# A chunked state-space scan: order of the mixture in VectorE's queue, size of a fill, and place of four products

## What is computed

```
acum = cumsum(a in the chunk)
seg = exp(where(tri, acum_i - acum_j, -inf))
cb = einsum('bnlgd,bnsgd->bnlsg', cc, bc)
y_diag = einsum('bnlsgr,bnsgrp->bnlgrp', cb[..., None] * seg, xc)
def step(state, inp):
    y_off = einsum('blgd,bgrpd,blgr->blgrp', c_i, state, exp(a_i))
    state = state * exp(a_last) + einsum('bsgd,bsgr,bsgrp->bgrpd', b_i, exp(a_last - a_i), x_i)
y = (y_diag + y_off) + d_skip[:, None] * xs
y = y * silu(z)        # and then an rmsnorm of each group of 512 columns
```

## Time and profile before

| | |
|---|---|
| median of 3 runs | 3552.8 us (3549.34 to 3553.31) |
| the profiled execution | 3547.36 us, of which the profile's span is 3545.5 us |
| share of busy time | TensorE 88%, VectorE 36%, ScalarE 28%, GpSimd 10% |
| mean granted TensorE clock | 0.936 of full |
| the preparing stage | about 2896 to 2917 us from the span's start |
| the scan | about 2917 to 3033.5 us |

### The profile page before, as it was taken

One profiled execution on the slowest core, in us unless ns is written; L12 is line 12 of the kernel. 1 busy time (PEld: TensorE's weight loads), 2 busy tenths in 40 slices (PEclk: granted clock), 3 DMA queues, 4 the chain that ended last, 5 costly groups with the idle time before them and its releaser, 6 DMA issues. The chain is left out here.

```text
span 3545.5 us, 45023 instructions
## 1 busy us (share of the span) xinstructions
PE 3116.1 (88%) x18464; PEld 2397.2 (68%) x18464; DVE 1277.1 (36%) x1505; ACT 990.9 (28%) x1456; POOL 362.8 (10%) x226
## 2 busy tenths in 40 slices
PE   6987658878758999998878999999999987789999
PEld 4975643333217888786776888788879764678887
DVE  3237651111124332335344332333232556433322
ACT  3125410000013221334224221422234443432222
POOL 2971000000000000100101000100010007110000
PEclk8999878988978999998899999999999999899999
DMA  6523268999973333220013332333323210323322
GB/s 229 166 88 144 63 275 343 427 428 428 428 284 83 95 96 106 72 83 16 2 60 83 95 95 103 88 95 95 103 68 102 83 38 2 101 55 95 95 96 88
DMA packets 301955, 487.06 MB, mean 137 GB/s; under 512 B 15618, under 2 KB 259805, under 8 KB 288495
## 3 DMA queue, kind: packets, MB, share of 16 engines
q1 hardware_dynamic: 297034, 467.35, 37.9%
q10 hardware_dynamic: 2468, 9.20, 0.6%
q0 software_dynamic: 2304, 8.39, 0.6%
HBM read 457.62 MB, written 27.28 MB: 137 GB/s over the span
## 5 line engine op out<-in xcount | busy, mean ns | idle before, releaser
L436 PE MATMUL psum_banks<-u_high,f_ffn_w_high 128*128 128x512 f32 x1408 | 548.6, 390 | 0.7 <-DVE f_ffn_w_low L2761 0.7
L437 PE MATMUL psum_banks<-u_low,f_ffn_w_high 128*128 128x512 f32 x1408 | 548.2, 389 | 0.0
L438 PE MATMUL psum_banks<-u_high,f_ffn_w_low 128*128 128x512 f32 x1408 | 548.1, 389 | 0.0
L2744 DVE TENSOR_TENSOR f_ffn_w_low<-weight_pieces,f_ffn_w_high 128x2048 fp32r<-128x2048 f32 x128 | 293.5, 2293 | 403.2 <-ACT f_ffn_w_high L2705 403.2
L2705 ACT ACTIVATE f_ffn_w_high<-weight_pieces 128x2048 fp32r<-128x2048 f32 x128 | 244.0, 1906 | 325.6 <-PE psum_banks L438 322.0
L436 PEld LDWEIGHTS psum_banks<-u_high,f_ffn_w_high 128*128 128x128 f32 x1408 | 264.6, 188 | 59.4 <-issue 4.2
L438 PEld LDWEIGHTS psum_banks<-u_high,f_ffn_w_low 128*128 128x128 f32 x1408 | 264.6, 188 | 55.0
L437 PEld LDWEIGHTS psum_banks<-u_low,f_ffn_w_high 128*128 128x128 f32 x1408 | 264.6, 188 | 54.4
L436 PE MATMUL psum_banks<-f_ffn_w_high,f_hidden_high 128*128 128x512 f32 x704 | 274.7, 390 | 3.6 <-issue 3.6
L438 PE MATMUL psum_banks<-f_ffn_w_high,f_hidden_low 128*128 128x512 f32 x704 | 274.0, 389 | 0.0
L437 PE MATMUL psum_banks<-f_ffn_w_low,f_hidden_high 128*128 128x512 f32 x704 | 273.9, 389 | 0.0
(11 more groups left out here) (651 smaller groups left out, 5572.0 us busy)
## 6 DMA issues: line engine op xcount, KB each, us to landing
expert_ring<-in_expert_w_gate SPq DMA_DIRECT2D x32, 2048.0 KB, 34.8
expert_ring<-in_expert_w_up SPq DMA_DIRECT2D x32, 2048.0 KB, 35.5
expert_ring<-in_expert_w_down SPq DMA_DIRECT2D x32, 2048.0 KB, 39.6
weight_pieces<-in_ffn_w_gate SPq DMA_DIRECT2D x88, 512.0 KB, 4.0
weight_pieces<-in_ffn_w_up SPq DMA_DIRECT2D x88, 512.0 KB, 5.3
weight_pieces<-in_ffn_w_down SPq DMA_DIRECT2D x88, 512.0 KB, 3.9
weight_pieces<-in_odd_w_in SPq DMA_DIRECT2D x20, 1024.0 KB, 5.4
mix_in_mod_w<-in_w_ada SPq DMA_DIRECT2D x32, 512.0 KB, 3.8
```

The costliest lines, as they stand in the source:

```text
L436: nc.tensor.matmul(out, lhs.high, rhs.high, start=start, stop=False, skip_group_check=True)
L437: nc.tensor.matmul(out, lhs.high, rhs.low, start=False, stop=False, skip_group_check=True)
L438: return nc.tensor.matmul(out, lhs.low, rhs.high, start=False, stop=stop, skip_group_check=True)
L2744: nc.vector.tensor_tensor(w.low[:, j], raw[:, j], w.high[:, j].bitcast(F32), ALU.subtract).then_inc(w_low, 1)
```

## The change

`own_x` isn't made by VectorE at the scan's start but by GpSimd in the preparing stage, into the free first half of the weight buffer. The fill at the scan's start clears only the first half's states. In VectorE's list of the scan, the mixture of unit 0 is made ahead of the loop and the mixture of unit n + 1 at the end of unit n, behind `advance(n, 1)`. The semaphore `own_ok` goes. The whole diff:

```diff
--- before.py
+++ after.py
@@ -3549,7 +3549,7 @@
 SSD_R = SSD_H // SSD_G
 
 
-def ssd_inputs(k, u_t, w_dt, b_dt, head, bc_t, xx, b_tok, xs, decay, ends):
+def ssd_inputs(k, u_t, w_dt, b_dt, head, bc_t, xx, b_tok, xs, decay, ends, own_x):
 
 
     nc = k.nc
@@ -3609,6 +3609,12 @@
                 last_mm = nc.tensor.matmul(k.ps[:, 2, (2 + half) * n:(3 + half) * n], pick, g, start=True, stop=True)
             last_mm.then_inc(sums_mm, 1)
             turns(range(15, JOBS))
+
+        @block.gpsimd
+        def _(pool):
+            for g in range(SSD_G):
+                nc.gpsimd.tensor_tensor(own_x[:, g], k.c("half_ident").unsqueeze(1).to_broadcast([P, SSD_R, CHUNK]),
+                                        head[:, 1, g * SSD_R:(g + 1) * SSD_R].unsqueeze(2).to_broadcast([P, SSD_R, CHUNK]), ALU.mult)
 
         @block.scalar
         def _(eng):
@@ -3674,7 +3680,7 @@
             nc.vector.tensor_tensor(flat(decay["rest"]), last[:], dt[:], ALU.mult).then_inc(small, 1)
 
 
-def ssd_scan(k, y, b_tok, bc_t, decay, ends, xs, skip, z, squares):
+def ssd_scan(k, y, b_tok, bc_t, decay, ends, xs, own_x, z, squares):
 
 
 
@@ -3687,8 +3693,8 @@
     with Stage(nc, "ssd") as s:
         state = s.sb("state", [P, SSD_G, 2, W])
         seg, mix = s.sb("seg", [P, 2, R, CHUNK]), s.sb("mix", [P, 2, R, CHUNK])
-        cb, own_x = s.sb("cb", [P, U, CHUNK]), s.sb("own_x", [P, SSD_G, R, CHUNK])
-        cb_mm, cb_ok, seg_mm, own_ok = s.sem("cb_mm"), s.sem("cb_ok"), s.sem("seg_mm"), s.sem("own_ok")
+        cb = s.sb("cb", [P, U, CHUNK])
+        cb_mm, cb_ok, seg_mm = s.sem("cb_mm"), s.sem("cb_ok"), s.sem("seg_mm")
         seg_ok, decayed, mixed, first_mm = s.sem("seg_ok"), s.sem("decayed"), s.sem("mixed"), s.sem("first_mm")
         upd_mm, diag_mm, off_mm, s_ok, y_ok = (s.sem(n) for n in ("update_mm", "diag_mm", "off_mm", "state_ok", "y_ok"))
         faded, faded_ok, scaled = s.sb("faded", [P, 2, W]), s.sem("faded_ok"), s.sem("scaled")
@@ -3832,10 +3838,7 @@
 
         @block.vector
         def _(v):
-            nc.vector.memset(state[:], 0.0).then_inc(s_ok, 1)
-            for g in range(SSD_G):
-                nc.vector.tensor_tensor(own_x[:, g], k.c("half_ident").unsqueeze(1).to_broadcast([P, R, CHUNK]),
-                                        skip[:, g * R:(g + 1) * R].unsqueeze(2).to_broadcast([P, R, CHUNK]), ALU.mult).then_inc(own_ok, 1)
+            nc.vector.memset(state[:, :, 0, :], 0.0).then_inc(s_ok, 1)
             v.wait_ge(cb_mm, 1)
             nc.vector.tensor_copy(cb[:, 0:U // 2, :].rearrange("p n i -> p (n i)"), k.ps[:, 6, :]).then_inc(cb_ok, 1)
 
@@ -3852,7 +3855,6 @@
                 v.wait_ge(seg_ok, n + 1)
                 if n == 0:
                     v.wait_ge(cb_ok, 2)
-                    v.wait_ge(own_ok, SSD_G)
                 if n >= 2:
                     v.wait_ge(diag_mm, n - 1)
                 nc.vector.tensor_tensor(mix[:, n % 2], seg[:, n % 2], cb[:, n, :].unsqueeze(1).to_broadcast([P, R, CHUNK]),
@@ -3868,12 +3870,14 @@
                 v.wait_ge(scaled, n + 1)
                 nc.vector.tensor_tensor(part(y, n), part(y, n), diag_bank(n), ALU.add).then_inc(y_ok, 1)
 
+            mixture(0)
             for n in range(U):
                 advance(n, 0)
-                mixture(n)
                 if n:
                     output(n - 1)
                 advance(n, 1)
+                if n + 1 < U:
+                    mixture(n + 1)
             output(U - 1)
 
 
@@ -3908,9 +3912,10 @@
             decay = {x: sb(s1, x, [P, NT, SSD_H])[:] for x in ("log", "shift", "exps", "rest")}
             ends = sb(s1, "ends", [P, 2, NT * SSD_H])
             xs = sb(s1, "xs", [P, NT, SSD_IN])
-            ssd_inputs(k, u_t, w_dt, b_dt[:, 0:1], head, bc_t, xx, b_tok, xs, decay, ends[:])
+            own_x = raw[:, 0, 0:SSD_G * SSD_R * CHUNK].rearrange("p (g r n) -> p g r n", g=SSD_G, r=SSD_R)
+            ssd_inputs(k, u_t, w_dt, b_dt[:, 0:1], head, bc_t, xx, b_tok, xs, decay, ends[:], own_x)
             u_open.close()
-            ssd_scan(k, y, b_tok, bc_t, decay, ends, xs, head[:, 1, :], z, group_ss[:])
+            ssd_scan(k, y, b_tok, bc_t, decay, ends, xs, own_x, z, group_ss[:])
         groups = [y[:, t, g * 512:(g + 1) * 512] for t in range(NT) for g in range(4)]
         norm_rows(k, "odd_groups", [(v, v) for v in groups], 512, sums=group_ss)
         y_t = split_sb(st, nc, "odd_y_t", [P, 16, SEQ])
```

## The result

The changed kernel takes 3523.1 us (median of 4 runs, 3519.8 to 3528.0) against 3553.1 for the kernel before, run beside it. The ratio is 0.9925, 95% interval 0.9913 to 0.9937, which is 26.6 us (22 to 31). The forecast was 3529.4, 23.4 us faster.

A forecast was written before the change was run, and what follows sets the result against it. A loop through several engines, with the mixture on it only by queue place, was taken to bound the scan. Gains 16.8 (period) + 5.3 (start) + 1.5 (end) - 0.2 (preparing stage) = 23.4 us, from 3552.8 to 3529.4; range 3522.8 to 3541.

The forecast's parts named there:

- its own signs: Scan: updates 5.2 to 5.4 us apart, diagonal products right behind the mask group, update 1 some 9.9 after GpSimd's first product.
- better than the forecast: Whole kernel: outcome with period 5.1 and start gain 5.8, 3525.6 us and below; chance 3%.
- What bounds the kernel: Steady scan: a 6.45 us loop through several engines; the mixture's 2.05 is on it only by its place in VectorE's queue.
- The period: Steady scan units: 5.3 us instead of 6.45, ends 5.1 and 6.01; gain 16.8 us over 14 periods.
- three loops: Steady scan: TensorE's work, GpSimd's queue and the loop through the mixture's new wait meet at 5.14 to 5.2 us.
- (a): Rival, steady scan: turns between VectorE and GpSimd cost whole instructions, 5.6 us a unit, 3533.6 us in all; chance 19%.
- (b): Rival, steady scan: GpSimd slow throughout, period 6.01 us, 3539.3 us in all; chance 9%.
- (c): Rival, steady scan: wait only exchanged, late mixture delays the state addition, period stays 6.45 us, 3545.5 in all; chance 6%.
- (d): Rival, scan: slower, TensorE's clock falls to half in the denser loop; 3569 us with 8 units at half clock; chance 3%.
- The start: Scan's start: half fill and four products gone, update 1 at 2927.2 instead of 2932.51; gain 5.3 us, bounds 4.3 and 5.8.
- The end: Scan's end, update 15 to last square: last state rows no longer wait through mixture 15; gain 1.5 us, bounds 1.2 and 2.1.
- The preparing stage: Stage before the scan: GpSimd's four products fit, but a turn delays a VectorE instruction; cost 0.2 us, bounds 0 and 1.0.

The follow-up runs named there:

- e1: Kernel before with only the order of VectorE's queue in the scan changed; whole fill and four products stay at the scan's start; 3525.8 us, ratio 0.9932.
- e6: Changed kernel with mixture n + 1 between the output and the second state addition of unit n, one place earlier in VectorE's queue; 3561.5 us, one run.
- e3: Kernel before with the new queue order and the half fill; the four products stay with VectorE at the scan's start; 3526.0 us, one run.
- e4: Changed kernel with the fill of all states again instead of half; 3520.3 us, one run.
- e5: Changed kernel without the gating on GpSimd, squares following the output directly (output not the reference's); 3516.4 us, one run.
- e8: Changed kernel with x times its decay to the end on ScalarE and the causal mask product from 16-bit copies; ratio 0.9918.
- e7: Changed kernel with x times its decay to the end made by ScalarE, eight instructions a unit, instead of GpSimd; ratio 0.9922.

## Why the prediction was right

The direction and the mechanism held; the sizes were a little low. The range held too, but only just: 3523.1 is 0.3 us above its low end. By its own signs the prediction was too cautious. It wanted updates 5.2 to 5.4 apart, and they are 5.13; the time lies in the outcome "better than the forecast", 3525.6 and below, to which it gave 3%. (That outcome's own terms, a period of 5.1 and a start of 5.8, add up to 3526.1.) By the ratio the gain is 26.6 us, which against the 3552.8 of the forecast gives 3526.2; the rest of the way down to 3523.1 is scatter, and that it ended 0.3 us inside the range is luck. The scan by itself gained 26.3 of a forecast 23.6. By its steps:

- **What bounds the kernel.** Right, and shown by e1: the mixture on the loop, 2.05 us of 6.45, was there by its place in the queue alone. e6 shows that the new place matters, not only that the old one was bad.
- **The period, 5.3 forecast, 5.13 measured.** The term that was mis-sized. GpSimd's queue was put at 5.14, which is what it is: fade 1.00, gating 1.23, and 1.46 and 1.45 with turns (forecast 1.00 + 1.24 + 1.45 + 1.45). TensorE was put at 5.14 to 5.2 and takes 4.94; I had taken 2.0 or more from the mask group to the diagonal products and it is 1.85, since groups that don't wait overlap their predecessor. The 1.08 for the diagonal products is 1.03. So not three loops met at the same length but one stood above the other two, and the 0.1 to 0.15 for latencies between them wasn't due: a queue that never runs dry (40.00 of 40.00) has none. 14 x (5.3 - 5.13) = 2.4 us of the miss.
- **Rivals.** (a), whole instructions as turns, 5.6, is out: the second instruction of a pair starts 1.45 to 1.46 after the first, 0.45 above 1.00. The rule of the Trainium skill ("SBUF — State Buffer", section "SBUF: two separate sides") that the lock is held for the whole instruction would give (a); the 0.45 is less than the instruction's 0.69, and the measurement decides. (b), 6.01, and (c), 6.45, are out: in each unit just two GpSimd instructions are held up, the other two are at 1.04 and 1.27. (d): the clock is 1.00 in the whole window.
- **The start, 5.3 forecast, 5.75 measured.** Within its bounds. Its parts, from run to run: the new order 1.67 (15.52 to 13.85, e1), the half fill 2.12 (to 11.73, e3), the blocks 1.96 (to 9.77). Taken the other way round, blocks first, they are 3.49 (13.85 to 10.36, e4) and the half fill 0.59: the products hold GpSimd's first instruction, and the fill sets when they end. I had put that instruction down to "fill and L3837"; e4 shows that the fill alone doesn't lengthen it.
- **The end, 1.5 forecast, 1.32 measured.** Right.
- **The preparing stage, 0.2 forecast.** The turn on the low half cost 0.07 (1.30 against 1.23). TensorE's projection didn't wait for it: it starts 3.29 after the stage's first matmul, 3.24 before. The stage was 0.8 us longer in the profiled execution, and that goes with TensorE's clock: in the first 6.0 us of the stage the granted clock was 0.57, against 0.72 before. The three shortest stages here, 20.54 to 20.58, all have 0.72, and one of them (e5) has GpSimd's products; the longest, 21.58 and 21.72 (e4, e8), have 0.53 and 0.57. Without GpSimd's products e3 took 21.13, at 0.61.
- **Outside the scan.** The stretch behind the scan took 510.6 to 515.2 us in these profiles, without order by kernel. The changed kernel's profile has one of the longest, 515.15, the kernel before 512.02. The stretch ahead of the preparing stage took 2891.2 to 2900.6 us; here the changed kernel's profile has the shortest, 2891.16, and the kernel before 2896.41. The measured 26.6 us by the ratio agree with the 26.3 of the scan; the difference of the two medians, 30.0, has some of this scatter in it.

No version here beats the changed kernel clearly: e7 and e8 come out at ratios 0.9922 and 0.9918 against 0.9925, intervals overlapping, for 0.9 and 2.5 us less in the scan.

## What to carry to other kernels

When no engine is full, walk one period from start to start until the sum is the period; a step that no one on that loop waits for is there only by its place in a queue, and can be moved behind the last instruction that the next round needs, and ahead of nothing that it would hold up (the changed kernel was 27 us faster than before; e6, with the mixture one place earlier, 13 slower, in one run). Then add up each engine's own queue with its turns at shared ports: the largest of the sums is the new period, and the second largest says how little the next improvement can bring (here 5.13 for GpSimd, 4.95 for TensorE and, in e8, again 4.95 for VectorE). Add nothing for latencies to a queue that never runs dry.

## What the runs showed of the hardware

- A VectorE instruction with both inputs in SBUF and a GpSimd one take turns, but overlap in part: each such VectorE instruction, 0.69 us alone, lengthened GpSimd's by 0.45 (1.49 busy instead of 1.04), and the VectorE one behind a GpSimd one took 1.41.
- VectorE products with both inputs in SBUF and no wait of their own, queued behind a fill, held GpSimd's instruction off before they began: it took 5.46 us with a long fill ahead of them, 3.32 with a short one, 1.04 beside a fill with none of them behind it (before, e3, e4). In both cases it ended 0.9 us after the first of them.
- The fill took 3.47 us for 4096 columns and 1.76 for 2048, so the second 2048 cost 1.71 us, 0.83 ns each.
- Two groups of small matmuls that don't wait start 0.92 us apart where each shows 1.09 to 1.10 busy, so the five groups' busy times (5.49 us) overstate a queue without waits (4.94) by 11%.
